# Last down projection with activations stationary: tokens on the partitions of the result, residual put in by transposes, last norm row by row

## The reference

```python
xn = rms_norm(x, ffn_norm_g[l])
gate, up = jnp.split(xn @ w_gate_up[l], 2, axis=-1)
x = x + (jax.nn.silu(gate) * up) @ w_down[l]     # (512, 2816) @ (2816, 1024)
return rms_norm(x, final_norm_g)                 # per token, over the 1024 columns
```

## Time and profile before

| | |
|---|---|
| median of 3 runs | 1447.9 us (1447.83 to 1449.83) |
| profiled execution: span from first to last instruction | 1442.4 us |
| what lies around the span (median less span) | 5.5 us |
| PE busy | 1383.9 us, 96% of the span, 6300 matmuls |
| DVE / ACT / POOL busy | 679.5 / 539.3 / 555.2 us |
| DMA | 124.42 MB, mean 86 GB/s |

### The profile page before, as it was taken

How to read it: one execution, slowest core, us unless ns; L and a number is a source line. 1 busy time by engine, 2 the same in 40 slices (tenths; PEclk the granted TensorE clock), 3 DMA queues, 4 the chain that set the end, 5 groups by cost and what they waited for, 6 DMA issues and landing times.

```text
span 1442.4 us, 16918 instructions
## 1 busy us (share of the span) xinstructions
PE 1383.9 (96%) x6300; PEld 1117.9 (77%) x6300; DVE 679.5 (47%) x1014; ACT 539.3 (37%) x883; POOL 555.2 (38%) x249
## 2 busy tenths in 40 slices
PE   7998999999999999997999999998989999999995
PEld 5876888887788888886887778886768888888884
DVE  7997436133723566666145733456653222221123
ACT  5223323223333565566333434446332322232220
POOL 3534544434353312214542531052344444444440
PEclk9999999999999999999999997889989999999998
DMA  4222322234233222221323320000223222222321
GB/s 159 91 87 98 114 88 98 92 102 147 74 104 103 85 74 66 67 74 45 131 88 102 107 85 30 30 30 30 74 88 101 88 87 102 89 100 88 103 73 58
DMA packets 36315, 124.42 MB, mean 86 GB/s; under 512 B 5120, under 2 KB 5120, under 8 KB 36000
## 3 DMA queue, kind: packets, MB, share of 16 engines
q1 hardware_dynamic: 34320, 116.93, 24.5%
q10 hardware_dynamic: 1936, 6.68, 1.3%
HBM read 115.14 MB, written 4.19 MB: 83 GB/s over the span
## 4 chain that ended last, share of the span: by engine, by line
PE 83%; issue 8%; DVE 4%; POOL 3%; ACT 1%; DMA 1%; DVEq 0%; POOLq 0%; SPq 0%; ACTq 0%
PE bank L1337 26%; PE bank L1338 25%; PE bank L1339 25%; POOL w_lo L426 3%; PE bank L1481 2%; PE bank L1455 1%; PE bank L1611 1%; PE bank L1469 1%; PE bank L1470 1%; DVE pool_xg L854 1%; PE bank L1361 0%; DVE ffn_xg L854 0%; DMA x<-x_in 0%; DVE prob_t L1099 0%; ACT y_hi L537 0%
## 5 line engine op out<-in xcount | busy, mean ns | idle before, releaser
L426 POOL TENSOR_TENSOR w_lo<-raw,w_hi 128x1024 fp32r<-128x1024 f32 x209 | 513.4, 2457 | 800.0 <-ACT w_hi L478 799.9
L478 ACT ACTIVATE w_hi<-raw 128x1024 fp32r<-128x1024 f32 x209 | 220.3, 1054 | 416.8 <-PE bank L1339 374.8
L1337 PE MATMUL bank<-ffn_xg,w_hi 128*128 128x512 f32 x352 | 141.3, 401 | 5.1 <-DVE ffn_xg L854 5.1
L1338 PE MATMUL bank<-ffn_xg,w_hi 128*128 128x512 f32 x352 | 140.2, 398 | 0.0
L1339 PE MATMUL bank<-ffn_xg,w_lo 128*128 128x512 f32 x352 | 140.0, 398 | 0.0
L1337 PE MATMUL bank<-pool_xg,w_hi 128*128 128x512 f32 x256 | 102.9, 402 | 15.6 <-DVE pool_xg L854 9.3
L884 DVE TENSOR_TENSOR x<-bank,x 128x512 f32<-128x512 f32 x24 | 16.6, 692 | 185.3 <-PE bank L1339 185.3
L1339 PE MATMUL bank<-pool_xg,w_lo 128*128 128x512 f32 x256 | 102.0, 398 | 0.0
L1338 PE MATMUL bank<-pool_xg,w_hi 128*128 128x512 f32 x256 | 101.9, 398 | 0.0
L1337 PE MATMUL bank<-y_hi,w_hi 128*128 128x512 f32 x256 | 101.3, 396 | 0.0
L1338 PE MATMUL bank<-y_lo,w_hi 128*128 128x512 f32 x256 | 101.2, 396 | 0.0
(11 more groups left out here) (334 smaller groups left out, 2932.9 us busy)
## 6 DMA issues: line engine op xcount, KB each, us to landing
raw<-stream SPq DMA_DIRECT2D x209, 512.0 KB, 3.4
rope_q<-turned_hl SPq DMA_DIRECT2D x64, 64.0 KB, 2.1
x<-x_in SPq DMA_DIRECT2D x4, 512.0 KB, 6.5
spill<-x ACTq DMA_DIRECT2D x1, 2048.0 KB, 6.3
x<-spill ACTq DMA_DIRECT2D x1, 2048.0 KB, 7.8
out<-x ACTq DMA_DIRECT2D x3, 256.0 KB, 2.8
out<-x SPq DMA_DIRECT2D x3, 256.0 KB, 2.1
ws_raw<-w_s ACTq DMA_DIRECT2D x1, 512.0 KB, 5.0
```

The source lines that it names most:

```text
L426: pool.tensor_tensor(w_lo[:, j % RING, :], raw[:, j % RAW, :], plain(w_hi[:, j % RING, :]), ALU.subtract).then_inc(tile_lo, 1)
L478: act.activation(w_hi[:, t % RING, :], raw[:, t % RAW, :], ACT.Copy).then_inc(tile_hi, 1)
L1337: pe.matmul(target, a_hi, b_hi, start=start, stop=False)
L1338: pe.matmul(target, a_hi, b_lo, start=False, stop=False)
```

## The change

The operands of the down projection change places. The 128 x 128 slice of `act_hi` or `act_lo` (128 hidden features by 128 tokens) is stationary and 512 columns of the weights move, so a bank holds 128 tokens on the partitions by 512 features. There are 4 blocks of tokens by 2 halves of the features, so 8 banks, and all 8 stay open over the whole product: the outer loop is now over the 22 hidden chunks `k`, the inner over the 8 banks. The stream's tile `k` is row chunk `k` of `w_down`, all 1024 columns. The number of matmuls of the product stays 22 x 8 x 3 = 528. The residual enters by 32 transposes (a matmul of a 128 x 128 piece of `x` with the identity) that write each bank first, four to a bank. The norm's sum is now over the free axis: ACT squares each bank with an accumulator; DVE adds two numbers for each token and takes the reciprocal, ACT the root, both on [128, 1], and DVE multiplies bank by root (a scalar for each partition) by a row of gains, which is loaded by a new DMA of 512 KB. `final_norm_2` leaves `cols`.

```diff
+            for k in range(FC):
+                t = TILE["ffn_down"] + k
+                wait_tile(0, t)
+                pe.wait_ge(act_lo_done, k + 1)
+                for b in range(NB):
+                    a = slice(P * b, P * (b + 1))
+                    for half in range(2):
+                        i = 2 * b + half
+                        target = bank[(4 + i) % 8]
+                        if k == 0:
+                            if i >= 4:
+                                pe.wait_ge(ffn_evac, 2 * FC - 8 + i + 1)
+                            for c in range(4):
+                                last = pe.matmul(target[:, P * c:P * (c + 1)], x[:, 4 * half + c, a], ident[:], start=c == 0, stop=False,
+                                                 is_transpose=True)
+                            if i == 0:
+                                last.then_inc(chunk_done, 1)
+                        last = three(target[:], act_hi[:, k, a], act_lo[:, k, a], *wblock(t, half, HALF_D), False, k == FC - 1)
+                        if k == FC - 1:
+                            last.then_inc(block_done, 1)
+                if k < FC - 1:
+                    last.then_inc(tile_used, 1)
```

ACT issues the gain row's DMA ahead of the norm that precedes the gate and up projection, and has a new end; DVE's end is new too:

```diff
             n = norm["ffn"]
+            act.dma_start(gain_row[:], rows_in[:, FOX_HEADS + 2 * D_SGU:]).then_inc(gain_in, 16)
...
             for k in range(FC):
                 split_tile("ffn_down", 0, k)
-                if done < DC and FC * (done + 1) <= 8 * (k - 1):
-                    final_chunk(done)
-                    done += 1
...
+            act.wait_ge(chunk_done, 1)
+            act.activation(fin_junk[:, 0:1], ones[:, 0:1], ACT.Sqrt).then_inc(fin_root, 1)
...
+            for b in range(NB):
+                for half in range(2):
+                    i = 2 * b + half
+                    act.wait_ge(block_done, i + 1)
+                    if i:
+                        act.wait_ge(fin_squared, i)
+                    act.activation(fin_junk[:], bank[(4 + i) % 8][:], ACT.Square,
+                                   accum_out=fin_sq[:, b, half:half + 1]).then_inc(fin_squared, 1)
+                    if b and half == 0:
+                        final_root(b - 1)
+            final_root(NB - 1)
+            store(act, 2 * NB - 2)
...
+            def final_block(b):
+
+                dve.wait_ge(fin_root, b + 2)
+                for half in range(2):
+                    c = slice(HALF_D * half, HALF_D * (half + 1))
+                    dve.scalar_tensor_tensor(y_out[:, b, c], bank[(4 + 2 * b + half) % 8][:], fin_inv[:, b:b + 1], gain_row[:, c],
+                                             ALU.mult, ALU.mult).then_inc(out_ready, 1)
+
+            for b in range(NB):
+                if b:
+                    final_block(b - 1)
+                dve.wait_ge(fin_squared, 2 * b + 2)
+                dve.tensor_scalar(fin_inv[:, b:b + 1], fin_sq[:, b, 0:1], fin_sq[:, b, 1:2], D * EPS, ALU.add,
+                                  ALU.add).then_inc(fin_summed, 1)
+                dve.wait_ge(fin_summed, b + 1)
+                dve.reciprocal(fin_inv[:, b:b + 1], fin_inv[:, b:b + 1]).then_inc(fin_prepared, 1)
+            final_block(NB - 1)
```

More of the change, by code:

```diff
@@ L76 @@
 RAW = 2
[L77 to L79 removed]
+HALF_D = D // 2
 AHEAD = RING - 1
@@ L358, in hi_units, with store @@
             return sum(o[0] != "rope" for o in UNITS[:UNIT[u] + 1])
[L360 to L367, removed]
+        def store(engine, i):
+            b, half = divmod(i, 2)
+            c = slice(HALF_D * half, HALF_D * (half + 1))
+            engine.wait_ge(out_ready, i + 1)
+            engine.dma_start(out[:, b, c], y_out[:, b, c]).then_inc(stored, 16)
         block = ctx.enter_context(nc.Block())
@@ L405, in _ @@
                 load(turn, j)
-            for k in OUT_ORDER[1::2]:
-                store(sp, k)
-            sp.wait_ge(stored, 16 * DC)
+            for i in (*range(2 * NB - 2), 2 * NB - 1):
+                store(sp, i)
+            sp.wait_ge(stored, 16 * 2 * NB)
         @block.gpsimd
@@ L815, in _, with final_root @@
             act_high(0, FC - 1)
[L816 to L826, removed]
             for k in range(FC):
                 split_tile("ffn_down", 0, k)
-                if done < DC and FC * (done + 1) <= 8 * (k - 1):
-                    final_chunk(done)
-                    done += 1
[L832 to L837, removed]
+            act.wait_ge(chunk_done, 1)
+            act.activation(fin_junk[:, 0:1], ones[:, 0:1], ACT.Sqrt).then_inc(fin_root, 1)
+            act.wait_ge(fin_root, 1)
+            def final_root(b):
+                act.wait_ge(fin_prepared, b + 1)
+                act.activation(fin_inv[:, b:b + 1], fin_inv[:, b:b + 1], ACT.Sqrt, scale=float(D)).then_inc(fin_root, 1)
+            for b in range(NB):
[10 more added lines that the diff above has]
+            store(act, 2 * NB - 2)
+            act.wait_ge(stored, 16 * 2 * NB)
             act.wait_ge(x_spilled, 16)
@@ L876, in take_bank @@
             def take_bank(stage, n, k):
[L878 to L883, removed]
+                dve.wait_ge(tile_used, TILE[stage] + 2 * (k + 1))
                 dve.tensor_tensor(x[:, k, :], bank[(k + 4) % 8][:], x[:, k, :], ALU.add).then_inc(n.x_ready, 1)
@@ L1318, in _ @@
             act_low(0, FC - 1)
[L1319 to L1330, removed]
+            dve.wait_ge(gain_in, 16)
+            def final_block(b):
+                dve.wait_ge(fin_root, b + 2)
+                for half in range(2):
+                    c = slice(HALF_D * half, HALF_D * (half + 1))
+                    dve.scalar_tensor_tensor(y_out[:, b, c], bank[(4 + 2 * b + half) % 8][:], fin_inv[:, b:b + 1], gain_row[:, c],
[9 more added lines that the diff above has]
+            final_block(NB - 1)
         @block.tensor
@@ L1784 @@
         outputs(TILE["mix_out"] + n, w_out[:, P * n:P * (n + 1)])
+    for k in range(FC):
+        put(TILE["ffn_down"] + k, 0, rows(w_down, k))
     for n in range(FC):
```

46 lines of the change are left out of this document (15 added, 31 removed).

## The result

The changed kernel takes **1439.42 us** (median of 4 runs, 1438.61 to 1440.18), the kernel before 1448.87 us on the same chip (4 runs, 1447.83 to 1450.0). The ratio is 0.9935, 95% interval 0.9921 to 0.9949: 9.4 us less, between 7.4 and 11.4. The forecast was 5.9 us less and 1442.0 us, range 1440.8 to 1445.2. The profiled execution took 1440.18 us, with a span of 1438.4.

The account below looks back on a forecast made before the run. PE was taken as the bound, busy 96% of the span, with 17.55 us nearly idle at the end. Terms +4.0 - 9.9 = -5.9 us took 1447.9 to 1442.0 us, range 1440.8 to 1445.2.

Parts of the forecast that it names:

- Part 1: Down projection's 528 matmuls: steps stay 0.23 us as in the second block's value projection, no new waits; cost 0.
- Part 2: 32 residual transposes on PE in the down projection: 0.50 us per group of four, eight groups, +4.0 us.
- Part 3: New end after the last matmul: 7.6 us long against 17.55, blocks at 2.0 us each; -9.9 us.
- Part 4: The rest: gain row's DMA issue falls in ACT's idle time, removed additions and squares were hidden behind PE; 0.
- Two bets: In the new end: squares reading PSUM cost the same as from SBUF, 0.75 us; products step 0.66 us with POOL at rest.
- the last part's "at the same time as now": Expected changed profile: no new ACT wait before the gate and up projection, which starts at the same time as now.
- The median of the runs is 5.5 us over the span and I keep that: Whole kernel: profiled span 1442.4 us, median taken as 1447.9, so the forecast is 1447.9 - 5.9 = 1442.0 us.
- The transposes eat: Rival, down projection: transposes at 0.27 us each end PE 8.7 us later, leaving -1.2 us, time 1446.7; chance 0.07.
- Granted clock: Rival, down projection: cycling banks lowers the clock, 1477 us, or only over the transposes, 1451.6; both together 0.06.
- The handshakes: Rival, the end: blocks cost 2.9 instead of 2.0 us, store 2.8, end 11.9, time 1446.3; chance 0.07.
- The range: Whole kernel's time: 1440.8 to 1445.2 us, meant to leave no more than 2 in 10 outside.

Follow-up runs that it names:

- after_x32: Changed kernel plus an unused tile of 32 bytes per partition behind `cols`, restoring the old operand addresses: 1441.49 us, ratio 0.9966 to the kernel before.
- no_residual: Changed kernel without the 32 transposes, so the residual is left out: 1435.51 us, ratio 0.9917 to the kernel before.
- rows_last: Changed kernel with all four blocks' products on DVE written behind all four small sums and reciprocals: 1440.3 us, ratio 0.9948 to the kernel before.
- before_x64: Kernel before plus 96 unused bytes per partition behind `cols`, putting `x` at 192 mod 256: 1430.87 us, ratio 0.9897 to the kernel before.

## Why the prediction was right or wrong

| term | forecast | measured |
|---|---|---|
| Part 1, 528 matmuls | 0 | -2.35 (527 steps of 0.2289 instead of 0.2333) |
| Part 2, 32 transposes | +4.0 | +3.6 |
| Part 3, the end | -9.9 | -10.0 |
| Part 4, gain row, hidden work | 0 | 0 |
| value projection of the second block | not looked at | -0.4 |
| value projection of `lat` | not looked at | -0.2 |
| sum | -5.9 | -9.3 |

**Part 1, "Cost 0", is the step that failed.** The wording was that number and shape stay and only operands change places, and that the step of 0.23 us is that of the value projection. In the kernel before it was: that projection's operands start 32 bytes apart mod 256, and so they do for the down projection in after_x32, which shows 0.2333. The analogy was right for the tiles where they were. What I did not work out is that an edit elsewhere, eight columns fewer in `cols`, moves them; 64 bytes apart gives 0.2289. after_x32 shows it: at the old addresses the changed product steps by 0.2333 and takes 3.5 us more than before, which is the transposes alone, as Part 1 and Part 2 have it. The other sentences of the part hold: PE has no gap in the stretch, so neither tiles nor activations nor `ffn_evac` are waited for.

**Part 2** is right in kind and 0.4 us high: 0.45 us a group instead of 0.50. The start-to-start distances show that four transposes take 0.36 us from the first start to the next matmul's, and the matmul behind them 0.31 instead of 0.23. By the Trainium skill's 275 ns ("TensorE: Matmul & The Clock Gate", PE-mode transpose) the estimate would be 8.8 us; no_residual shows 3.6, so that is the time of one, not what one adds in a row.

**Part 3** holds to 0.2 us, step by step: the first square at E - 4.7 (forecast E - 4.9), a first pair of products at E - 2.35 (forecast E - 2.4), a period of 2.0 us (2.0), the last product's end at E + 5.05 (5.1), the store 2.1 us to landing (2.1), DVE the slow one. Two bets in it came true: that a square read from PSUM costs as from SBUF (0.78 us from one to the next, forecast 0.75), and that the products go at 0.66 a step with POOL at rest, which the single rows above show for the old end too.

**Part 4** holds. Timeline of ACT and its queue in the changed kernel, in answer to the earlier trace rows:

```profile
1011.56 1.35 ACT L784 ACTIVATE sgu<-bank,cols 128x512 fp32r<-128x512 f32 x2 [0.96 <-PE bank L1667]
1012.23 0.33 ACTq L786 DMA_DIRECT2D gain_row<-lines  x1
1015.09 1.06 ACT L471 ACTIVATE w_hi<-raw 128x1024 fp32r<-128x1024 f32 x1 [2.18 <-PE bank L1337]
```

The issue falls into the idle time: ACT's wait for PE is 2.18 us, it was 2.16. The start of the product came 4.7 us late, against the last part's "at the same time as now", but so did this stage already, by 4.35 us, ahead of the DMA.

**"The median of the runs is 5.5 us over the span and I keep that"** was a wrong reading. In every execution with its own span shown, time less span is 1.7 to 1.9 us (1440.18 and 1438.4, for one). The profiled execution of the kernel before was one of the quick ones of a kernel whose spans scatter over 6 us. It did no harm, because it was kept on both sides: 1447.9 less the 9.3 of the stages is 1438.6, 0.8 us from the measured median.

**The rivals** all fall. The transposes eat 3.6 us and not 8.7. Granted clock is 1.00 throughout 22 rounds over eight banks and the eight groups of transposes (the row of busy time above). The Trainium skill's A second HAM failure mode (same page) tells of a clock that swings in such a pattern, with PE idle for moments between the groups; in this trace PE is never idle and the clock does not swing. The handshakes cost a block 2.0 us and not 2.9. That rival's sum was wrong too: products at 1.03 add 0.74 to a block and the waits 0.4, so a block would be 3.1 us, the end 12.9 and the time 1447.3; and 1.03 was no price of a product, as the single products under rows_last show.

**The range** was too narrow for a reason that can be named: every term in it was a term of the diff's instructions. None stood for the steps of 527 matmuls, where 2% is 2.4 us. How far the median lies below the range is partly scatter: the interval of the difference is 4 us wide, and what the traces show is 3.0 us of matmul steps beyond the forecast out of the 3.5 measured.

## What to carry to other kernels

Before pricing a matmul stretch at "unchanged", work out where its operands start after the edit, mod 256; an edit of a small tile moves all that are allocated behind it. Where PE is the bound with 512 moving columns, try paddings before anything else: 32 bytes here took 1.3% off the kernel before, more than the whole change did. And a norm whose tokens stand on the partitions turns its reciprocal and root into steps on one column, so a product that ends in one is worth transposing if the residual's transposes (0.45 us per bank) are cheaper than the tail that goes.

## What the hardware showed that I had not expected

Matmuls of 128 x 128 by 512 columns, back to back with a new stationary operand each time, at granted clock 1.00, step by 0.2267 us when moving and stationary operands start at the same place mod 256 bytes, by 0.2290 when the moving one starts 64 bytes further, and by 0.2325 to 0.2342 at every other multiple of 32. The stationary operand 64 bytes further gives the long step, so it is not symmetric. With 256 columns the order is another one and 0 is among the slowest (0.1198 us, against 0.1137 for 64 in before_x64's gated projection), with 128 there are no differences. Why this is so stays open: no run here looks behind the steps, and I have tried shifts only in multiples of 32. That no more than the difference counts was shown for two common shifts, 32 and 96, and for 32 with 288.

Transposes in float32 of 128 x 128 step by 0.11 us, and go in between matmuls of another type without idle time; the first matmul behind a group takes 0.08 us more to the next start.

While POOL ran its two products in the old end, DVE's stepped by 1.67 to 1.77 us instead of 0.66.
